# Layer 0's last stage: middle-channel products in four column groups, with one copy and four stores

## The chip, the cores and the metric

The kernel runs on one core of one Trainium2 chip. The metric is device time in microseconds (us) from launch to end; lower is better. The core has a matrix engine (TensorE, PE in the profile), which reads SBUF and writes PSUM, a vector engine (DVE), a scalar engine (ACT), GpSimd (POOL) and a sync engine (SP). SP and POOL are the two that issue DMA transfers here. Each engine runs its own instructions in order; semaphores join them.

## The reference

The model has two layers. Layer 0 ends with an expert-choice channel mixer; layer 1 begins with a Fourier mixer and a linear map `w_f`:

```python
def fourier_mixer(h, w_f):
    b, n, d = h.shape
    hg = h.astype(jnp.float32).reshape(b, n, FNET_GROUPS, d // FNET_GROUPS)
    f = jnp.fft.fftn(hg, axes=(1, 3), norm='ortho').real.reshape(b, n, d).astype(h.dtype)
    return jnp.einsum('bnd,de->bne', f, w_f)

def expert_choice_ffn(x, w_router, w_gate, w_up, w_down):
    b, n, d = x.shape
    t = x.reshape(b * n, d)
    cap = CAPACITY_FACTOR * (b * n) // N_EXPERTS
    aff = jax.nn.softmax(jnp.einsum('td,de->te', t, w_router).astype(jnp.float32), axis=-1)
    g, idx = lax.top_k(aff.T, cap)
    xe = t[idx]
    ...
```

The kernel moves the transform over channels to the weights: it multiplies the channel transform into `w_f` once, long before layer 1 wants it. The channels stand in `GROUPS` = 4 groups of `GW` = 256. A transform of 256 real channels has cosine and sine rows, and one middle row (frequency 128) whose factors are +1, -1, +1, ... over 16. Its products with `w_f` are the "middle channels' mixing weights", `w_f_mid`: one row of D = 1024 numbers for each group, 4 x 1024 in all.

## The kernel before

The program is a row of stages, each a block in which every engine has its own list, with a barrier of all engines between blocks. The stage of the change is `mix0` (function `output_and_choice`). It does layer 0's output projection, the normalised tokens `xh`, the router's logits, and the choice of tokens by each expert (DVE's `rounds`: repeatedly the eight largest of each row). PE has spare time while DVE chooses, and makes the mixing weights there.

`mixing_weight_products` lists these products in order: 16 of 512 columns into `w_f_mixed` (cosine and sine, for four groups and two halves of the columns), and then 2 into `w_f_mid`, one for each half of the columns. Each of the last two is a sum of four matmuls, one for each group g, whose stationary operand `alt_c[:, g, :]` has 4 columns (only column g is not zero) and whose moving operand is `folded[0][:, g, ...]`, 512 columns. The result is 4 rows x 512 in PSUM partitions 0 to 3.

For every product n the same three steps follow one another:
- PE (`mixing_weights`, L1562 to L1572) waits until the product before the last has been copied out, multiplies into one of the two banks of `acc[0]`, and raises `w_full`.
- ACT (`mixing_weights_kept`) waits for `w_full` and for the store that last used the buffer, copies the bank into `stage[n % 4]` (L1652), and raises `w_kept`.
- POOL (L1527 to L1529) waits for `w_kept` and issues a store of that buffer to DRAM, which raises `w_out[n % 4]` when it has landed.

The order at the end of the stage is fixed by the code. PE runs products 11 to 17 and then `choice.turn_lists` (L1255 to L1260), which transposes the chosen lists when DVE's `write_lists` (L1362 to L1366) has raised `lists_ready`. DVE's `write_tables` (L1371 to L1382) turns these into token numbers and raises `tables_ready`; L1382 is its last instruction. POOL, after the 18 stores, waits for `tables_ready` in `fetch_first` and issues two gathers, of the first expert's prompt tokens (L1388) and sample tokens (L1389). Then POOL waits for the landing of all stores (`w_out`), and its list is over. After the barrier the experts' stage begins (`experts`): PE turns the gathered tokens (L1949, L1962), and SP asks for the second expert's weights (L1799).

Two places elsewhere in the program are of use for comparison. Layer 1's mixing stage has a helper `middle` (L2304) which multiplies a stationary operand of one column with 256 moving columns for each quarter of the output columns, with quarter q at PSUM partition 32 q. Layer 1 also has the same chain of lists, tables and gathers at its end, with no stores in POOL's list before it.

Of the kernel before, what the change touches and what calls it, by code (L numbers as in the profile page):

```python
# [29 lines left out]
ACT = mybir.ActivationFunctionType  # L30
# [21 lines left out]
GROUPS = 4  # L52
GW = D // GROUPS
# [5 lines left out]
BANK = 512  # L59
# [46 lines left out]
def wait(eng, sem, value):  # L106

    if not isinstance(value, int) or value > 0:
        eng.wait_ge(sem, value)
# [1315 lines left out]
def output_and_choice(nc, t, per, room, weights):  # L1425
# [4 lines left out]
    with Stage(nc, "mix0") as s:  # L1430
# [10 lines left out]
        acc = [s.ps(f"acc{u}", 2) for u in range(2)]  # L1441
        choice = Choice(s, t, per, 0, [lg[0][:], lg[1][:]], tp, False)
        raw = [s.sb(f"raw{u}", [P, 2, BANK]) for u in range(2)]
        folded = [x[1][:].rearrange("p k f -> p (k f)").rearrange("p (g e) -> p g e", g=GROUPS) for x in (weights.gate, weights.up)]
        stage = [s.sb(f"stage{u}", [P, BANK]) for u in range(4)]
        cos_c, sin_c, odd_c = s.sb("cos_c", [P, HG]), s.sb("sin_c", [P, HG]), s.sb("odd_c", [1, HG])
        alt_c = s.sb("alt_c", [P, GROUPS, GROUPS])
        raw_in, fold_done, chan_in = s.sems("raw_in", 2), s.sem("fold_done"), s.sem("chan_in")
        w_full, w_kept, w_out = s.sem("w_full"), s.sem("w_kept"), s.sems("w_out", 4)
        w_products = list(mixing_weight_products(t["w_f_mixed"], t["w_f_mid"], folded, cos_c[:], sin_c[:], odd_c[:], alt_c[:]))  # L1450
        N_W = len(w_products)

        gate_in, a_in, x_in = s.sem("gate_in"), s.sems("a_in", 2), s.sems("x_in", 2)
# [17 lines left out]
        with nc.Block() as block:  # L1471
# [53 lines left out]
            @block.gpsimd  # L1525
            def _(pool):
                for n, (dst, _) in enumerate(w_products):  # L1527
                    pool.wait_ge(w_kept, n + 1)
                    pool.dma_start(dst, stage[n % 4][0:dst.shape[0], :]).then_inc(w_out[n % 4], 16)  # L1529
                for u in range(2):  # L1530
                    pool.wait_ge(xh_out[u], 16 * NT // 2)
                choice.fetch_first(pool, weights)
                for u in range(4):
                    pool.wait_ge(w_out[u], 16 * ((N_W + 3 - u) // 4))

            @block.tensor
            def _(pe):
                def product(m, half, lo, hi):
                    u = m % 2
                    if half == 0 and lo == 0:  # L1540
                        if m:
                            pe.wait_ge(a_in[u], 32 * ((m + 1) // 2))
                        wait(pe, gated, m - 1)
                    for k in range(lo, hi):
                        last = pe.matmul(acc[u][:, half * BANK:(half + 1) * BANK], a_t[u][:, k, :],
                                         room.row(k)[:, half * BANK:(half + 1) * BANK], start=(k == 0), stop=(k == KD - 1))
                    if half == 1 and hi == KD:
                        last.then_inc(full, 1)

                def turn(m):  # L1550
                    u = m % 2
                    pe.wait_ge(xh_ready, m + 1)
                    for b, kept in ((0, v_kept), (1, a_kept)):
                        wait(pe, kept, m)
                        for j in range(4):
                            k = 4 * b + j
                            last = pe.transpose(tp[b][:, j * P:(j + 1) * P], xh[u][:, k * P:(k + 1) * P], per.ident[:])
                        last.then_inc(tp_full, 1)

                def router(m):  # L1560
                    pe.wait_ge(v_kept, m + 1)
                    pe.wait_ge(a_kept, m + 1)  # L1562
                    choice.route(pe, m // 4, m % 4, xh_t[m % 2])

                def mixing_weights(lo, hi):
                    for n in range(lo, hi):
                        dst, terms = w_products[n]
                        wait(pe, w_kept, n - 1)
                        for m, (stationary, moving) in enumerate(terms):
                            last = pe.matmul(acc[0][0:dst.shape[0], (n % 2) * BANK:(n % 2 + 1) * BANK], stationary, moving,  # L1570
                                             start=(m == 0), stop=(m == len(terms) - 1))
                        last.then_inc(w_full, 1)  # L1572

                pe.wait_ge(room.w_o_in, 32)
                pe.wait_ge(room.first_in, 32)
                product(0, 0, 0, KD)
                product(0, 1, 0, KD)
                choice.make_bias(pe)
                for m in range(1, NT):
                    product(m, 0, 0, KD)  # L1580
                    if m < NT - 1:
                        turn(m - 1)
                        product(m, 1, 0, 4)
                        router(m - 1)
                        product(m, 1, 4, 6)
                        if m in (4, 8):
                            choice.turn_batch(pe, m // 4 - 1)
                        product(m, 1, 6, KD)
                    else:
                        choice.turn_affinities(pe, 1)  # L1590
                        product(m, 1, 0, 4)
                        turn(m - 1)
                        product(m, 1, 4, KD)
                        router(m - 1)
                pe.wait_ge(gated, NT - 1)
                pe.wait_ge(chan_in, 64)
                pe.wait_ge(fold_done, 4 * GROUPS)
                mixing_weights(0, 8)
                turn(NT - 1)
                router(NT - 1)  # L1600
                choice.turn_batch(pe, 2)
                mixing_weights(8, 11)
                choice.turn_affinities(pe, 0)
                mixing_weights(11, N_W)
                choice.turn_lists(pe)

            @block.scalar
            def _(act):
# [38 lines left out]
                def mixing_weights_kept(lo, hi):  # L1647
                    for n in range(lo, hi):
                        rows = w_products[n][0].shape[0]
                        act.wait_ge(w_full, n + 1)  # L1650
                        wait(act, w_out[n % 4], 16 * (n // 4))
                        act.activation(stage[n % 4][0:rows, :], acc[0][0:rows, (n % 2) * BANK:(n % 2 + 1) * BANK], ACT.Copy).then_inc(w_kept, 1)  # L1652
# [10 lines left out]
                choice.keep_batch(act, 2)  # L1663
                choice.exponentials(act, 0)
                mixing_weights_kept(8, N_W)

            @block.vector
            def _(dve):
# [66 lines left out]
                choice.write_tables(dve, ch)  # L1735


def mixing_weight_products(w, w_mid, folded, cos_c, sin_c, odd_c, alt_c):

    for half in range(2):  # L1740
        e = slice(half * BANK, (half + 1) * BANK)
        for g in range(GROUPS):
            yield w[0][g, :, e], [(cos_c, folded[0][:, g, e]), (odd_c, folded[1][0:1, g, e])]
            yield w[1][g, :, e], [(sin_c, folded[1][:, g, e])]
    for half in range(2):
        e = slice(half * BANK, (half + 1) * BANK)
        yield w_mid[:, e], [(alt_c[:, g, :], folded[0][:, g, e]) for g in range(GROUPS)]


class Buffers:  # L1750
# [1054 lines left out]
```

## Time and profile before

| what | value |
|---|---|
| median of 3 runs | 2194.54 us (2191.77 to 2197.46) |
| the profiled execution | 2183.69 us, of which the span from first to last instruction is 2181.9 us |
| PE busy / DVE / ACT / POOL | 2027.1 / 863.0 / 470.3 / 154.6 us |
| end of the stage `mix0` | about 1051.2 us into the span (POOL's last gather) |
| first PE work of the experts' stage | 1056.67 us |

All times in rows are of the profiled execution, in us from the start of its span. A float32 matmul of the program stands as two instructions in the trace, each with a weight load (PEld) ahead of it. A timeline row gives start, length, engine, line, operation, output<-inputs, shape and count; the bracket at its end says how long the engine was idle before, and what ended that. The length of a PE row that merges several matmuls runs to the end of the last one, and the next row can begin before that, since matmuls are pipelined.

### The profile page before, as it was taken

Reading aid. Unit: us, or ns where it says so; the run is one execution under the profiler, and the core shown is the slowest. Engines: PE = TensorE matmul, PEld = TensorE weight load, DVE = VectorE, ACT = ScalarE, POOL = GpSimd, SP = SyncE. Lnnn points to the kernel's source line nnn. Section 1 sums busy time; section 2 is a strip of 40 time slices with the busy share of each in tenths; the row PEclk is TensorE's granted clock in tenths of the full one; section 3 lists DMA queues with packets and bytes.
Section 4 is the critical chain, followed back from the end, with each engine's and each line's share of the span. In section 5 each row is a group of like instructions: output and inputs, shape, how many; then the busy total and the mean of one; then the engine's idle time right before and its main releaser. Section 6 shows DMA issues by size and latency. Waiting matters only on the chain. (4 is left out here: it accounts for less than half of the span.)

```text
span 2181.9 us, 27610 instructions
## 1 busy us (share of the span) xinstructions
PE 2027.1 (93%) x11515; PEld 1430.7 (66%) x11515; DVE 863.0 (40%) x1810; ACT 470.3 (22%) x929; POOL 154.6 (7%) x147
## 2 busy tenths in 40 slices
PE   5999999979999999999799999995998499999998
PEld 2776777755666665443587878783444387878785
DVE  2245445455666664337222222222657522222221
ACT  1222222126665563113000000001222200000000
POOL 0000000000000000001111111111000101111110
PEclk9999999989999999998899999997898699999999
DMA  9201111048444323753767878776221797878782
GB/s 354 94 29 44 43 43 41 25 104 290 176 172 168 136 98 122 264 173 135 268 234 258 305 258 305 248 227 216 99 97 58 277 330 251 302 260 302 261 283 61
DMA packets 159085, 404.29 MB, mean 185 GB/s; under 512 B 12561, under 2 KB 30664, under 8 KB 152818
## 3 DMA queue, kind: packets, MB, share of 16 engines
q1 hardware_dynamic: 142370, 344.30, 43.9%
q0 software_dynamic: 16592, 58.24, 9.3%
q8 instruction: 91, 1.49, 0.3%
q14 instruction: 32, 0.26, 0.0%
HBM read 339.46 MB, written 63.05 MB: 184 GB/s over the span
## 5 line engine op out<-in xcount | busy, mean ns | idle before, releaser
L1970 PE MATMUL experts_gu<-experts_h_t,shared_w_gate 128*128 128x160 f32 x2048 | 303.0, 302 | 4.1 <-issue 4.1
L1970 PEld LDWEIGHTS experts_gu<-experts_h_t,shared_w_gate 128*128 128x128 f32 x2048 | 289.1, 192 | 19.1 <-issue 19.1
L1970 PE MATMUL experts_gu<-experts_h_t,shared_w_up 128*128 128x160 f32 x2048 | 299.7, 300 | 0.0
L1970 PEld LDWEIGHTS experts_gu<-experts_h_t,shared_w_up 128*128 128x128 f32 x2048 | 285.8, 191 | 0.0
L2046 DVE TENSOR_TENSOR experts_hid<-experts_act,experts_gu 128x160 f32<-128x160 f32 x128 | 41.2, 322 | 478.9 <-ACT experts_act L2035 478.9
L1994 PE MATMUL experts_dn<-shared_w_down,experts_hid 128*128 128x512 f32 x512 | 225.9, 594 | 0.0
L523 PE MATMUL proj_cv<-proj_h_t,proj_w_in 128*128 128x256 f32 x960 | 212.4, 379 | 2.6 <-DVE proj_h_t L720 2.6
L2035 ACT ACTIVATE experts_act<-experts_gu 128x160 f32<-128x160 f32 x128 | 38.8, 303 | 813.0 <-PE experts_gu L1970 813.0
L523 PEld LDWEIGHTS proj_cv<-proj_h_t,proj_w_in 128*128 128x128 f32 x960 | 181.8, 191 | 28.6 <-issue 4.7
L1994 PEld LDWEIGHTS experts_dn<-shared_w_down,experts_hid 128*128 128x128 f32 x512 | 94.9, 190 | 113.7 <-issue 113.7
L1008 PE MATMUL attn_sc<-attn_keys_s,attn_q_s 96*128 96x512 f32 (+1 forms) x384 | 154.7, 539 | 3.8 <-DVE attn_pr_t L1141 2.8
L1123 DVE TENSOR_REDUCE attn_least<-attn_sc 128x1 f32<-128x512 f32 (+1 forms) x192 | 109.7, 599 | 101.7 <-PE attn_sc L1008 101.7
L1008 PEld LDWEIGHTS attn_sc<-attn_keys_s,attn_q_s 96*128 96x128 f32 x384 | 67.7, 189 | 90.8 <-issue 64.3
L1074 ACT ACTIVATE attn_pr<-attn_sc,attn_neg 128x1280 f32<-128x1280 f32 x64 | 84.9, 1327 | 128.0 <-DVE attn_neg L1125 128.0
L1081 ACT ACTIVATE attn_pr<-attn_pr,attn_inv 128x512 f32<-128x512 f32 (+2 forms) x144 | 106.3, 785 | 3.5 <-DVE attn_inv L1131 3.5
L516 PE MATMUL proj_lp<-proj_w_in,proj_h_t 128*128 128x384 f32 (+1 forms) x320 | 93.6, 452 | 3.3 <-DVE proj_h_t L720 3.3
L516 PEld LDWEIGHTS proj_lp<-proj_w_in,proj_h_t 128*128 128x128 f32 x320 | 61.6, 193 | 33.3 <-issue 4.9
L1141 DVE COPY attn_pr_t<-attn_sc 128x512 f32<-128x512 f32 x128 | 82.6, 686 | 1.7 <-PE attn_sc L1022 1.7
L1022 PE MATMUL attn_sc<-all_ident,attn_pr 128*128 128x128 f32 x640 | 80.7, 273 | 0.1
L1022 PEld LDWEIGHTS attn_sc<-all_ident,attn_pr 128*128 128x128 f32 x640 | 74.0, 141 | 6.8 <-ACT attn_pr L1081 0.5
L1043 PE MATMUL attn_o<-attn_pr_t,attn_vals_s 128*64 128x128 f32 x1280 | 76.9, 275 | 0.6 <-DVE attn_pr_t L1141 0.6
L1043 PEld LDWEIGHTS attn_o<-attn_pr_t,attn_vals_s 128*64 128x64 f32 x1280 | 69.2, 137 | 6.0 <-issue 5.2
(412 smaller groups left out, 2111.0 us busy)
## 6 DMA issues: line engine op xcount, KB each, us to landing
shared_w_gate<-w_gate_l SPq DMA_DIRECT2D x32, 2048.0 KB, 9.5
shared_w_up<-w_up_l SPq DMA_DIRECT2D x32, 2048.0 KB, 17.3
shared_w_down<-w_down_l SPq DMA_DIRECT2D x32, 2048.0 KB, 22.3
attn_w_mod<-w_mod_l SPq DMA_DIRECT2D x40, 1024.0 KB, 6.6
proj_w_in<-w_in_l SPq DMA_DIRECT2D x3, 2048.0 KB, 19.8
proj_x<-x POOLq DMA_DIRECT2D x10, 512.0 KB, 4.2
shared_w_down<-x SPq DMA_DIRECT2D x10, 512.0 KB, 4.5
layer_room_a<-w_mod_l SPq DMA_DIRECT2D x4, 1024.0 KB, 10.2
```

Source lines behind the costliest of these rows:

```text
L516: last = pe.matmul(lp[:, base:base + hi - lo], h_t[n // 2 % 2][:, k, cols], w_in[:, k, lo:hi], start=(k == 0), stop=(k == KD - 1))
L523: last = pe.matmul(cv[bank][:, j * PAIR:(j + 1) * PAIR], w_in[:, k, base + j * P:base + (j + 1) * P], h_t[p % 2][:, k, :], start=(k == 0), ...
L1008: pe.matmul(sc[b][:, lo:hi], q_s[tile % 2][:, h * P:(h + 1) * P], keys_s[:, h, lo:hi], start=True, stop=True).then_inc(s_full, 1)
L1022: last = pe.transpose(sc[b][:, m * P:(m + 1) * P], pr[b][:, m * P:(m + 1) * P], per.ident[:])
L1043: last = pe.matmul(o_ps[VH * side:VH * (side + 1), base:base + width], vals[:, m, h * VH:(h + 1) * VH], pr_t[n % 4][:, m * width:(m + 1) * ...
L1074: act.activation(pr[b][:], sc[b][:, 0:K], ACT.Exp, bias=neg[b][:, 0:1], scale=-1.0, accum_out=total[b][:, 0:1]).then_inc(p_ready, 1)
L1081: act.activation(pr[b][:, lo:hi], pr[b][:, lo:hi], ACT.Copy, scale=inv[b][:, a:a + 1]).then_inc(p_scaled, 1)
L1123: ch.add(dve.tensor_reduce(least[:, k:k + 1], sc[b][:, lo:hi], AX.X, ALU.min))
L1141: dve.tensor_copy(pr_t[n % 4][:, lo:hi], sc[n % 2][:, lo:hi]).then_inc(v_kept, 1)
L1970: last = pe.matmul(gu[j % 2][:, m * SLOTS:(m + 1) * SLOTS], w[u][:, k, j * P:(j + 1) * P], h_t[u][:, k, :], start=(k == 0), stop=(k == KD ...
L1994: last = pe.matmul(dn[half][:], hid[i][:, k, 0:CAP_S], wd[i][:, k, cols], start=(k == 0), stop=(k == KF - 1))
L2046: dve.tensor_tensor(hid[e % BATCH][:, j, :], act_sb[j % 2][:], gu[j % 2][:, SLOTS:2 * SLOTS], ALU.mult).then_inc(hid_ready, 1)
```

## The change

The two products of `w_f_mid` leave the list of products, which now has 16. PE makes the middle channels in a function of its own, `middle_weights`, after the 16 and still ahead of `turn_lists`. The output columns are cut into four quarters of 256. For each group g there are four matmuls, one for each quarter q, that write PSUM partitions 32 q to 32 q + 3, columns 0 to 255 of one bank. ACT copies all 128 partitions x 256 columns in one instruction; POOL issues four stores of 4 x 256, each raising the new semaphore `mid_out`, and waits for `mid_out` at the very end of its list.

```diff
-        w_full, w_kept, w_out = s.sem("w_full"), s.sem("w_kept"), s.sems("w_out", 4)
-        w_products = list(mixing_weight_products(t["w_f_mixed"], t["w_f_mid"], folded, cos_c[:], sin_c[:], odd_c[:], alt_c[:]))
+        w_full, w_kept, w_out, mid_out = s.sem("w_full"), s.sem("w_kept"), s.sems("w_out", 4), s.sem("mid_out")
+        w_products = list(mixing_weight_products(t["w_f_mixed"], folded, cos_c[:], sin_c[:], odd_c[:]))
...
                     pool.dma_start(dst, stage[n % 4][0:dst.shape[0], :]).then_inc(w_out[n % 4], 16)
+                pool.wait_ge(w_kept, N_W + 1)
+                for q in range(4):
+                    pool.dma_start(t["w_f_mid"][:, q * GW:(q + 1) * GW], stage[N_W % 4][32 * q:32 * q + GROUPS, 0:GW]).then_inc(mid_out, 16)
...
                     pool.wait_ge(w_out[u], 16 * ((N_W + 3 - u) // 4))
+                pool.wait_ge(mid_out, 64)
...
+                def middle_weights():
+                    wait(pe, w_kept, N_W - 1)
+                    for g in range(GROUPS):
+                        for q in range(4):
+                            last = pe.matmul(acc[0][32 * q:32 * q + GROUPS, (N_W % 2) * BANK:(N_W % 2) * BANK + GW], alt_c[:, g, :],
+                                             folded[0][:, g, q * GW:(q + 1) * GW], start=(g == 0), stop=(g == GROUPS - 1), skip_group_check=True)
+                    last.then_inc(w_full, 1)
...
                 mixing_weights(11, N_W)
+                middle_weights()
                 choice.turn_lists(pe)
...
                 mixing_weights_kept(8, N_W)
+                act.wait_ge(w_full, N_W + 1)
+                act.wait_ge(w_out[N_W % 4], 16 * (N_W // 4))
+                act.activation(stage[N_W % 4][:, 0:GW], acc[0][:, (N_W % 2) * BANK:(N_W % 2) * BANK + GW], ACT.Copy).then_inc(w_kept, 1)
...
-    for half in range(2):
-        e = slice(half * BANK, (half + 1) * BANK)
-        yield w_mid[:, e], [(alt_c[:, g, :], folded[0][:, g, e]) for g in range(GROUPS)]
```

On PE, at the end of the stage, before (names are tiles; the shape is that of the output):

```order
501 L1570 MATMUL mix_acc<-shared_w_gate,mix_alt_c 4x512 x8
502 L1255 MATMUL mix_tp<-all_ident,mix_best 128x48
503 L1255 MATMUL mix_tp<-all_ident,mix_lists 128x48 x3
504 L1257 MATMUL mix_tp<-all_ident,mix_at_pf 32x16
505 L1260 MATMUL mix_lg<-all_ident,mix_at_pf 32x4 x4
```

and now, at the same place on PE:

```order
501 L1582 MATMUL mix_acc<-shared_w_gate,mix_alt_c 4x256 x16
502 L1255 MATMUL mix_tp<-all_ident,mix_best 128x48
503 L1255 MATMUL mix_tp<-all_ident,mix_lists 128x48 x3
504 L1257 MATMUL mix_tp<-all_ident,mix_at_pf 32x16
505 L1260 MATMUL mix_lg<-all_ident,mix_at_pf 32x4 x4
```

Nothing has moved around the middle products; 8 matmuls of 512 columns have become 16 of 256, still ahead of the lists (L1255).

On POOL, from the last stores to the two gathers, before:

```order
34 L1529 DMA w_f_mixed<-mix0_stage2 128x512
35 L1529 DMA w_f_mixed<-mix0_stage3 128x512
36 L1529 DMA w_f_mid<-mix0_stage0 4x512
37 L1529 DMA w_f_mid<-mix0_stage1 4x512
38 L1388 DMA shared_w_down3<-xh_prompt,all_at_p4 128x1024
39 L1389 DMA shared_w_down3<-xh_sample,all_at_s 128x1024
```

and now, on POOL:

```order
34 L1529 DMA w_f_mixed<-mix0_stage2 128x512
35 L1529 DMA w_f_mixed<-mix0_stage3 128x512
36 L1532 DMA w_f_mid<-mix0_stage0 4x256 x4
37 L1388 DMA shared_w_down3<-xh_prompt,all_at_p4 128x1024
38 L1389 DMA shared_w_down3<-xh_sample,all_at_s 128x1024
```

Four small stores stand where two stood, and the gathers still come right behind them.

## Rows read from the trace of the kernel before

**Rows 1.** The page, part 1: busy time, share and instructions by engine.

```profile
PE 2027.1 (93%) x11515; PEld 1430.7 (66%) x11515; DVE 863.0 (40%) x1810; ACT 470.3 (22%) x929; POOL 154.6 (7%) x147
```

**Rows 2.** Timeline of DVE, end of `mix0`: start, length, engine, line, operation.

```profile
1039.93 0.22 DVE L1366 CAST mix_lists<-mix_at 48x128 f32<-48x128 uint32 x1
1046.78 0.36 DVE L1371 COPY mix_merge<-mix_tp 128x192 f32<-128x192 f32 x1 [6.62 <-PE mix_lg L1260]
...
1047.84 0.17 DVE L1382 TENSOR_TENSOR all_at_s<-mix_moved,mix_merge 128x16 uint32<-128x16 f32 x1
```

**Rows 3.** Timeline of PE, end of `mix0` and start of the experts.

```profile
1038.95 7.03 PE L1570 MATMUL mix_acc<-shared_w_gate,mix_alt_c 128*4 128x512 f32 x16
1045.91 0.26 PE L1255 MATMUL mix_tp<-all_ident,mix_best 48*128 48x48 f32 x1
...
1056.67 1.94 PE L1949 MATMUL experts_tp<-all_ident,shared_w_down 128*128 128x128 f32 x8 [9.96 <-PEq L1471]
```

**Rows 4.** Timeline of POOL, end of `mix0`.

```profile
1039.94 0.54 POOL L1529 DMA_DIRECT2D w_f_mixed<-mix_stage  x1 [0.52 <-ACT mix_stage L1652]
1043.46 0.52 POOL L1529 DMA_DIRECT2D w_f_mid<-mix_stage  x1 [2.97 <-ACT mix_stage L1652]
1046.89 0.52 POOL L1529 DMA_DIRECT2D w_f_mid<-mix_stage  x1 [2.91 <-ACT mix_stage L1652]
1048.88 1.03 POOL L1388 DMA_INDIRECT shared_w_down<-xh_prompt,all_at_p  x1 [1.46 <-DVE all_at_s L1382]
1050.21 0.97 POOL L1389 DMA_INDIRECT shared_w_down<-xh_sample,all_at_s  x1 [0.30 <-issue]
```

**Rows 5.** Timeline of ACT: the copy of the first middle product.

```profile
1042.58 0.59 ACT L1652 ACTIVATE mix_stage<-mix_acc 4x512 f32<-4x512 f32 x1 [2.93 <-PE mix_acc L1570]
```

**Rows 6.** Layer 1's `middle` (L2304): PE's timeline, then one line's ns min/median/max.

```profile
1664.98 1.04 PE L2304 MATMUL mix_banks<-shared_w_down 128*1 128x256 f32 x16
1665.96 0.61 PE L2304 MATMUL mix_banks<-mix_w_mid,shared_w_down 4*1 4x256 f32 x8
...
L2304 PE MATMUL mix_banks<-shared_w_down x32: 377/378/380, 1661.9 to 1665.7; 128*1 128x256 f32 x32
```

**Rows 7.** ACT's copies of 128 x 256 from PSUM, elsewhere: ns min/median/max.

```profile
L1088 ACT ACTIVATE attn_pr_t<-attn_sc x64: 372/373/383, 511.7 to 841.3; 128x256 f32<-128x256 f32 x64
```

**Rows 8.** Timelines of POOL and DVE elsewhere: small DMAs in a row, waits for DVE.

```profile
5.15 2.03 POOL L202 DMA_DIRECT2D proj_mod_bias<-b_mod_l  x4
...
37.72 0.75 DVE L710 TENSOR_SCALAR proj_xh<-proj_x,proj_rstd 128x1024 f32<-128x1024 f32 x1
...
38.77 0.54 POOL L468 DMA_DIRECT2D proj_x<-x  x1 [26.16 <-DVE proj_xh L710]
...
1719.84 0.18 DVE L1382 TENSOR_TENSOR all_at_s<-mix_moved,mix_merge 128x16 uint32<-128x16 f32 x1
...
1720.82 0.98 POOL L1388 DMA_INDIRECT shared_w_down<-xh_prompt,all_at_p  x1 [22.01 <-DVE all_at_s L1382]
```

**Rows 9.** DMA issues: engine, operation, count, KB each, median us to landing.

```profile
proj_mod_bias<-b_mod_l POOLq DMA_DIRECT2D x4, 4.0 KB, 8.3
...
w_f_mid<-mix_stage POOLq DMA_DIRECT2D x2, 8.0 KB, 1.7
```

**Rows 10.** Windows: us, engines' busy us (instructions), granted PE clock, DMA share, GB/s.

```profile
4.00:9.00 5.00, 0.41 (x2) 0.28 (x2) 0.74 (x3) 1.71 (x4) 3.18 (x6) 1.00 0.72 265
...
1038.95:1045.85 6.90, 6.90 (x17) 1.31 (x16) 1.10 (x5) 1.18 (x2) 1.54 (x3) 1.00 0.19 77
...
1067.00:1068.00 1.00, 1.00 (x5) 1.00 (x5) 0.00 (x0) 0.00 (x0) 0.00 (x0) 0.50 1.05 414
1068.00:1070.00 2.00, 2.00 (x16) 2.00 (x15) 0.00 (x0) 0.07 (x1) 0.00 (x0) 0.97 1.03 398
...
1728.40:1738.00 9.60, 7.55 (x33) 6.73 (x34) 4.45 (x7) 1.24 (x1) 3.01 (x3) 0.54 0.85 282
```

**Rows 11.** Timeline of SP's queue: the experts' stage asks for weights.

```profile
1057.49 0.42 SPq L1799 DMA_DIRECT2D shared_w_gate<-w_gate_l  x1
```

More of the change, by code:

```diff
@@ L1735, in _, with mixing_weight_products @@
                 choice.write_tables(dve, ch)
-def mixing_weight_products(w, w_mid, folded, cos_c, sin_c, odd_c, alt_c):
+def mixing_weight_products(w, folded, cos_c, sin_c, odd_c):
     for half in range(2):
```

## Prediction

> **What bounds the kernel now.** PE is busy 93% of the span [rows 1], but a share over the whole span does not say what the end of one stage waits for. So I read the timelines of the engines at the end of `mix0` side by side, from DVE's last choice to the barrier.
>
> DVE has the chosen lists ready at 1039.93 + 0.22 = 1040.15. Its next instruction begins at 1046.78: it was idle for 6.62 us, and PE released it [rows 2]. PE had not been waiting in that time: it was in the middle products, 16 instructions from 1038.95, and began to turn the lists only at 1045.91 [rows 3]. So from 1040.20 to 1045.91 the choice waits for nothing but PE's order of work. Behind that, in one chain, come the tables, whose last instruction ends at 1047.84 + 0.17 = 1048.01 [rows 2], POOL's two gathers at 1048.88 and 1050.21, the second ending at 1051.18 [rows 4], and 5.49 us after that PE's first work for the experts at 1056.67 [rows 3]. SP asks for the experts' next weights only then, at 1057.49 [rows 11], so the transfers of the next stage move with its start. I found nothing at a fixed time there that would eat a shift; what the end of `mix0` gains should be gained at the end of the kernel.
>
> **PE: the products.** Before, 16 instructions of 512 columns take 1045.91 - 1038.95 = 6.96 us, with the clock fully granted [rows 3, 10]: 0.43 us each and about 0.1 us for the change to the next kind of matmul. 256 columns are half of that, 0.214 us. The new code has 32 instructions of 256 columns, so the same number of columns in all. If the four column groups did not overlap it would win nothing.
>
> Layer 1's `middle` shows the overlap in the same form: four quarters, 256 columns, outputs at partitions 0, 32, 64, 96. Sixteen instructions occupy PE from 1664.98 to 1665.96, 0.98 us [rows 6], where sixteen in turn would need 16 x 0.214 = 3.43. So four run in the time of one, and 0.98 - 4 x 0.214 = 0.12 us is the change of kind. Thirty-two are eight such rounds: 8 x 0.214 + 0.12 = 1.84 us. Their start stays 1038.95, since the wait ahead of them is for the same copy as before. PE then turns the lists at 1040.79, after the lists are ready at 1040.15. Gain at this point: 1045.91 - 1040.79 = 5.12 us.
>
> The Trainium skill ("TensorE: Matmul & The Clock Gate", Part 3, measured speedup) gives less for column packing: three tiles ran 2.38 times as fast, not three times. At the same share four tiles would give 3.17, hence an estimate of 6.86 / 3.17 + 0.12 = 2.28 us in place of 1.84, and a total gain 0.4 us smaller. The row of this kernel shows the full factor; I go by the row.
>
> **DVE.** The turned lists come 5.12 us earlier, so the tables end at 1048.01 - 5.12 = 1042.89.
>
> **ACT: the copy.** Two copies of 0.59 us [rows 5] become one. The last product starts at 1038.95 + 7 x 0.214 + about 0.01 = 1040.46 and lasts 0.378 [rows 6], to 1040.84; ACT began 0.04 us after the end of the first middle product before, so now at 1040.88. 128 x 256 from PSUM took 0.373 us elsewhere [rows 7]: to 1041.25. Its extra wait is for the store of product 12, issued long before; no row shows ACT held by it.
>
> **POOL: the stores, which are the new neighbour of the path.** POOL began a store 0.29 us after the copy ended (1042.58 + 0.59 = 1043.17, then 1043.46) [rows 4, 5], so the first of the four begins at 1041.54; the last old-style store ended at 1040.48 [rows 4], so POOL is free. One middle store took 0.52 us, and four DMAs of 4 KB in a row took 2.03 us [rows 4, 8]. Four stores: 4 x 0.522 = 2.09, to 1043.63. That is 0.74 us after the tables are done, so the gathers no longer wait for DVE, but for POOL's own stores.
>
> What lies between POOL's last store and its first gather, when the semaphore is up already, no row shows. The lower bound is the gap between the two gathers, 0.30 us [rows 4]. The upper one is the whole way from DVE's last instruction to the gather, 0.87 here (1048.01 to 1048.88), and 0.80 in layer 1, where POOL had been idle for 22 us [rows 2, 4, 8]: this way is no effect of queued stores. I take 0.57: of the 0.87 a DVE signal to a plain POOL DMA takes 0.30 (37.72 + 0.75 = 38.47, to 38.77) [rows 8], and a signal that has come already costs nothing.
>
> **The sum.** First gather at 1043.63 + 0.57 = 1044.20, against 1048.88: 4.7 us earlier. With 0.30 it is 4.95, with 0.87 it is 4.4. If the stores were hidden it would be the 5.12 of PE. POOL's last wait, for `mid_out`, is hidden behind the gathers: the last store is issued at 1043.11, a middle store landed 1.7 us after its issue [rows 9], that is 1044.8, and the second gather ends at 1044.20 + 1.03 + 0.30 + 0.97 = 1046.50. If that cover is gone it costs what rival 2 says.
>
> The profiled execution took 2183.69 us (span 2181.9); less 4.7 it is 2179.0 (span 2177.2). It lies 10.9 us under the median shown, so the difference, not its own time, is carried over: 2194.54 - 4.7 = **2189.8 us**. That is 0.21%. About 0.3%, 6.6 us, is what a measurement of this kernel can tell from no change, so the likeliest case is a real gain too small for that bound.
>
> **Rival 1: the column groups do not overlap here.** Then PE needs 32 x 0.214 = 6.86 us as before, and the change does not do what it says. The lists are turned at 1045.91 as before, but the copy now waits for all the products: the last matmul ends at 1045.97, the copy at 1046.38, the four stores at 1048.76, the gather begins at 1049.33, 0.45 us later than before: 2195.0. For it: the stationary operand has four columns here and one in `middle`. Against it: sixteen instructions in 0.98 us in the same form.
>
> **Rival 2: the landing of the stores ends the stage; slower.** POOL must see `mid_out` at 64 before the barrier. Four POOL transfers of 4 KB issued in a row, the very size of the new stores, have a landing of 8.3 us elsewhere [rows 9]. With that the last store lands at 1043.11 + 8.3 = 1051.41, 0.23 us after the old end of POOL's list at 1051.18: 2194.8. The gain begins to shrink at a landing of 1046.50 - 1043.11 = 3.4 us, and is a loss from 8.1 us. For it: same queue, same size. Against it: these 8.3 us stand where the DMA engines are busy 0.72 of the time, at the middle stores it is 0.19 [rows 10], and 8 KB stores from the same place landed in 1.7.
>
> **Rival 3: the clock of the experts' first matmuls.** PE begins the experts at half clock, and the granted clock reads 0.50 to 1068.0 and 0.97 over the next 2 us [rows 10]; so it rises about 11.4 us after 1056.67. In the same place of layer 1 the window of 9.60 us that begins with PE's restart has 0.54 [rows 10]: only some 8% of it, 0.8 us, can be at full clock, so the rise is 8.8 us after the restart. The two differ by 2.6 us. At half clock that is worth 1.3 us. PE is idle for about the same time before the restart in both kernels, so the step itself stays; but when it comes may shift with the start. Earlier, the gain is 6.0 (2188.5); later, 3.4 (2191.1).
>
> **How the numbers follow.** Forecast (a gain of 4.4 to 5.1) 0.74; rival 3 in either direction 0.16, the earlier rise the likelier since this trace has the later one; rival 1 0.04; rival 2 0.06. The three runs of before lie 5.7 us apart, so a median may lie some 2.8 us off. The low end is rival 3's 2188.5 less 2.8, about 2185.5; the high end takes in rivals 1 and 2 at 2195.0 and a little scatter, 2195.5. Faster by over 0.3% needs a gain of 6.6 us: the earlier clock with some scatter, or the forecast with much of it, 0.12. Slower by over 0.3% has no mechanism here that is large enough, only scatter behind rivals 1 and 2: 0.02. Within 0.3%: 0.86.
>
> **What the profile of the changed kernel would show.** For PE's step: the middle products about 1.84 us long from their start to the first matmul of the lists. If it is near 6.9, rival 1 is right. For DVE: the wait ahead of L1371 falls from 6.6 to about 1.5 us. For POOL: four stores back to back, 2.0 to 2.1 us, and the first gather 0.3 to 0.9 us behind the last of them, its idle time put down to POOL's own issue and not to DVE. If it still comes 0.8 us behind DVE's last instruction, the stores were hidden. For rival 2: a landing of `w_f_mid` above 3.4 us, and a longer stretch than 5.5 us from the end of the second gather to PE's first matmul of the experts. For rival 3: where the clock reads 1.00 after that restart. The prediction is wrong if this shift of about 4.7 us stands at the barrier but not at the end of the span.

## Result and the profile after

Four executions of each kernel gave a median of 2182.89 us (2179.72 to 2183.62) for the changed one and 2196.0 us (2191.77 to 2198.36) for the one before: a ratio of 0.994 with a 95% interval of 0.992 to 0.9959. That is 13.1 us, where the prediction had 4.7, and 2182.89 lies 2.6 us under the low end of its range. Yet the two profiled executions have almost the same span, 2181.9 us before and 2181.3 us after. Both need an explanation, and it is the same one. With more executions (experiments 1, 2 and 5) the means are 2190.5 us for 80 executions of before and 2185.2 us for 28 of the changed kernel, a difference of 5.3 us with a 95% interval of 2.9 to 7.7. Without the first four of each it is 4.5 us (1.8 to 7.3). One execution of experiment 7 took 3610.0 us, at a mean granted clock of 0.554, and is left out of its ratio.

First the end of `mix0` in the changed kernel. Timeline of DVE, to be held against [rows 2]:

```profile
1044.48 0.22 DVE L1366 CAST mix_lists<-mix_at 48x128 f32<-48x128 uint32 x1
1046.22 0.36 DVE L1371 COPY mix_merge<-mix_tp 128x192 f32<-128x192 f32 x1 [1.51 <-PE mix_lg L1260]
...
1047.28 0.18 DVE L1382 TENSOR_TENSOR all_at_s<-mix_moved,mix_merge 128x16 uint32<-128x16 f32 x1
```

Timeline of PE, against [rows 3]:

```profile
1043.51 1.91 PE L1582 MATMUL mix_acc<-shared_w_gate,mix_alt_c 128*4 128x256 f32 x32
1045.35 0.26 PE L1255 MATMUL mix_tp<-all_ident,mix_best 48*128 48x48 f32 x1
...
1056.48 1.94 PE L1962 MATMUL experts_tp<-all_ident,shared_w_down 128*128 128x128 f32 x8 [10.33 <-PEq L1471]
```

Timelines of ACT and POOL, against [rows 4, 5]:

```profile
1045.48 0.38 ACT L1681 ACTIVATE mix_stage<-mix_acc 128x256 f32<-128x256 f32 x1 [1.27 <-PE mix_acc L1582]
...
1046.15 2.03 POOL L1532 DMA_DIRECT2D w_f_mid<-mix_stage  x4 [1.11 <-ACT mix_stage L1681]
1048.49 1.02 POOL L1388 DMA_INDIRECT shared_w_down<-xh_prompt,all_at_p  x1 [0.30 <-issue]
1049.82 0.96 POOL L1389 DMA_INDIRECT shared_w_down<-xh_sample,all_at_s  x1 [0.30 <-issue]
```

DMA issues of the stretch 1036 to 1060, median us to landing last, against [rows 9]:

```profile
w_f_mid<-mix_stage POOLq DMA_DIRECT2D x4, 4.0 KB, 1.6
```

The middle products take 1045.35 - 1043.51 = 1.84 us in place of 6.96. DVE waits 1.51 us for the turned lists in place of 6.62. The four stores take 2.03 us, and the first gather begins 0.30 us behind the last of them; the bracket puts that gap down to POOL's own issue and no longer to DVE.

Times of day don't compare here, since the products begin at 1043.51 and not at 1038.95. Counted from their start, the first gather comes after 1048.49 - 1043.51 = 4.98 us, against 9.93 before; the experts' first matmul after 12.97, against 17.72. The stage has become 4.75 us shorter, but in this execution it began 4.56 us later than in the profiled execution of before. That is why the two spans agree.

Why it began later is not the change's doing: the lists of instructions are the same up to this place. The granted clock differs. Windows of before, then the same of the changed kernel (columns as in [rows 10], the granted clock is the third number from the end):

```profile
460.00:520.00 60.00, 45.35 (x209) 29.57 (x208) 34.88 (x79) 28.47 (x68) 0.00 (x0) 0.86 0.86 228
840.00:880.00 40.00, 36.01 (x175) 18.02 (x173) 11.40 (x21) 4.73 (x9) 0.00 (x0) 1.00 0.55 172
1000.00:1036.00 36.00, 31.99 (x95) 11.72 (x94) 31.87 (x78) 13.20 (x22) 6.57 (x13) 0.81 0.49 175
```

```profile
460.00:520.00 60.00, 46.07 (x199) 31.42 (x201) 34.88 (x81) 25.79 (x64) 0.00 (x0) 0.80 0.83 222
840.00:880.00 40.00, 36.00 (x197) 19.66 (x195) 11.91 (x25) 7.94 (x14) 0.00 (x0) 0.91 0.52 166
1000.00:1036.00 36.00, 31.98 (x107) 12.72 (x106) 33.30 (x80) 13.03 (x22) 5.41 (x10) 0.86 0.46 168
```

The clock has two levels, so a mean of 0.80 in 60 us means 24 us at half rate, against 16.8 at 0.86. The changed kernel's execution has 7.2 us more half-rate time in each of the first two windows and 3.6 us less in the third: 10.8 us more, in which PE does at most 5.4 us less work. The stage began 4.56 us later.

The other traces, of both kernels, bear this out. In the clock's records of the eight traces in which PE's order ahead of the middle products is the same, the products start at 1038.33 with 37.5 us of half-rate time ahead of them, 1038.95 with 41.0 (before), 1041.57 with 44.4, 1043.51 with 51.2 (the changed kernel's first), 1043.94 with 54.6 (before again), 1046.88 and 1047.07 with 61.4, and 1049.80 with 64.9: in one order, whichever the kernel.

### The profile page after: what moved, and what is told of

It reads as the page before. It is cut to its first block and busy times, and to the rows that moved or that the text cites. A ratio compares the mean times of both kernels' runs of the same rounds, so it can differ in the third digit from the quotient of the medians.

```text
span 2181.3 us, 27642 instructions
## 1 busy us (share of the span) xinstructions
PE 2028.1 (93%) x11531; PEld 1433.6 (66%) x11531; DVE 862.9 (40%) x1810; ACT 469.6 (22%) x928; POOL 155.0 (7%) x149
```

## Experiments

Theory A: the change is worth 4.7 to 5 us, at the end of `mix0`, and what is more than that between the first medians comes from where half-rate stretches fell in those executions. Theory B: it is worth some 13 us in every execution, by something outside that place.

**1. The kernel before, unchanged, against itself.**

> The kernel before, unchanged, timed against itself, for a second trace and the granted clock of more executions. Theory A (the change is worth 4.7 to 5 us at the end of mix0, and the rest of the 13 us between the medians is where the clock's half-rate stretches happened to fall in the executions compared): executions of this one kernel spread over 8 us or more, between about 2183 and 2198 us, and the longer ones have the lower mean clock, some 0.955 to 0.960 against 0.965 in the profile of before. Theory B (the change is worth some 13 us in every execution, by something outside the end of mix0): the executions lie close to 2196, and the 2183.69 of the profiled one stays the exception. Ratio to the kernel before under both: 1.000.

Measured: ratio 0.9999 (0.9981 to 1.0017). Its 12 executions reach from 2184.29 to 2197.92 us, the 35 of the kernel before beside them from 2183.57 to 2196.96. So one kernel spreads over 13 to 14 us within a set, and the 2183.69 of the first profile is the lower edge of that, not a thing apart. Its trace shows the end of `mix0` as in [rows 2 to 4], 4.99 us later:

```profile
1043.94 7.03 PE L1570 MATMUL mix_acc<-shared_w_gate,mix_alt_c 128*4 128x512 f32 x16
1050.90 0.26 PE L1255 MATMUL mix_tp<-all_ident,mix_best 48*128 48x48 f32 x1
...
1061.47 1.94 PE L1949 MATMUL experts_tp<-all_ident,shared_w_down 128*128 128x128 f32 x8 [9.77 <-PEq L1471]
```

What theory A expected came, its detail on the clock too: sorted by mean granted clock, the executions of both kernels fall in order (76 of before and 28 of the changed kernel that have a listed clock; correlation of time and clock -0.89 and -0.95):

| mean clock | before: executions, mean us | changed: executions, mean us |
|---|---|---|
| 0.957 to 0.959 | 6, 2195.7 | 8, 2192.8 |
| 0.960 | 17, 2195.5 | 3, 2188.6 |
| 0.961 to 0.962 | 13, 2190.5 | 7, 2183.4 |
| 0.963 | 19, 2188.1 | 3, 2182.6 |
| 0.964 | 15, 2186.4 | 4, 2178.5 |
| 0.965 to 0.967 | 6, 2185.3 | 3, 2177.2 |

**2 and 5. The changed kernel, unchanged, twice more.**

> The changed kernel, unchanged, timed once more. Theory A: the ratio comes back between 0.994 and 1.000, nearest to 0.998 (4.7 us of 2195), and at equal mean clock it is 4 to 5 us below the kernel before. Theory B: again 0.994, and also at equal clock some 13 us below.

> The changed kernel once more, unchanged, for twelve more executions and a third trace. Theory A (the gain is made at the end of mix0 alone, and half-rate stretches of PE's clock ahead of the stage make the rest of the difference): from the start of the middle products to the experts' first matmul 12.8 to 13.0 us (17.5 and 17.7 in the two traces of before, 12.8 and 13.0 in those of after), wherever the stage begins; the stage begins the later, the more half-rate time lies ahead of it (1038.95 with 41 us of it, 1047 with 61). Ratio 0.996 to 0.999. Theory B (13 us in every execution): 0.994.

Measured: 0.9975 (0.9955 to 0.9996) and 0.9983 (0.9962 to 1.0004), that is 5.5 and 3.7 us; the second interval takes in 1, and the medians of experiment 5 alone (2189.99 against 2188.6) show no gain. The 13 did not come back. The third trace is a long one (span 2190.3) whose stage begins only at 1049.80, and still it has the same lengths (the experts' first matmul 12.75 us after the products' start; 12.83 in experiment 2's trace):

```profile
1049.80 1.91 PE L1582 MATMUL mix_acc<-shared_w_gate,mix_alt_c 128*4 128x256 f32 x32
1051.64 0.26 PE L1255 MATMUL mix_tp<-all_ident,mix_best 48*128 48x48 f32 x1
...
1062.55 1.94 PE L1962 MATMUL experts_tp<-all_ident,shared_w_down 128*128 128x128 f32 x8 [10.11 <-PEq L1471]
```

Two traces of before have 17.72 and 17.53, three of the changed kernel 12.97, 12.83 and 12.75: 4.8 us by the means. From there to the end of the span it is 1125.2 and 1127.6 us before, 1124.8, 1125.1 and 1127.8 after: these lengths scatter by 3 us, and within that nothing of the gain is given back or added.

One length does not repeat. In this third trace DVE waits 5.68 us for the turned lists and not 1.51:

```profile
1052.51 0.36 DVE L1371 COPY mix_merge<-mix_tp 128x192 f32<-128x192 f32 x1 [5.68 <-PE mix_lg L1260]
```

There PE, at half rate from 1020 to 1047 by the clock's records, is still at the 16 products ahead of the middle ones when DVE has its lists at 1046.83. The end of the stage hangs on PE in either case, which is why lengths counted from the start of the middle products compare and DVE's wait does not.

The expectation of experiment 2 missed in one point: at equal mean clock the table's rows differ by 2.9 to 8.1 us, not by 4 to 5. One slope for both kernels puts the difference at 6.8 us (6.0 to 7.7). The mean clock also counts half-rate time in which PE is idle and which costs nothing. Between the start of the middle products and the experts' first matmul that is 5.6 and 5.2 us in the traces of before and 7.7, 7.5 and 8.5 in those of the change, by the clock's records. So at equal mean clock the changed kernel has some 2.5 us less of the half-rate time that does cost. By an estimate from these figures, 2.5 us at half rate are worth 1.25 us, and 4.8 + 1.25 = 6.05. What is left is less than 1 us, and the interval reaches down to it.

**3. No overlap: the loops exchanged.**

```diff
-                    for g in range(GROUPS):
-                        for q in range(4):
+                    for q in range(4):
+                        for g in range(GROUPS):
```

> The changed kernel with the two loops of the middle products exchanged: the four groups of one quarter follow one another in one column group, so neighbours can't overlap; same number of instructions, same copy, same four stores. Both theories: the middle products take 6.9 us in place of 1.84, and the first gather comes 9.2 to 9.7 us after DVE's lists (8.7 in before, 3.8 in after), since the copy now waits for all 32. Theory A: 0.2 to 0.8 us slower than before, ratio 1.000. Theory B with a cause in the stores or in the one copy and not in the overlap: still well below 1, 0.995 to 0.997.

Measured: ratio 0.9981 (0.9965 to 0.9998).

```profile
1046.88 4.50 PE L1582 MATMUL mix_acc<-shared_w_gate,mix_alt_c 128*4 128x256 f32 x32
1051.31 0.26 PE L1255 MATMUL mix_tp<-all_ident,mix_best 48*128 48x48 f32 x1
...
1054.42 1.02 POOL L1388 DMA_INDIRECT shared_w_down<-xh_prompt,all_at_p  x1 [0.30 <-issue]
```

The expectation failed: 4.43 us, not 6.9. Windows of 0.2 us of these matmuls alone show why (the first number with an x is PE's busy time, and the x counts the instructions in flight in the window):

```profile
1047.26:1047.46 0.20, 0.20 (x2) 0.09 (x1) 1.00 0.00 0
...
1048.26:1048.46 0.20, 0.20 (x6) 0.07 (x3) 1.00 0.94 389
...
1050.66:1050.86 0.20, 0.20 (x3) 0.07 (x1) 1.00 0.00 0
```

At first one instruction follows another, with two in a window (each lasts 0.379 us and the next begins 0.21 us after it); in the middle there are up to six. The length tells the same: 4.43 us are about 20 steps of 0.214 and the change of kind, where 32 in turn would need 32 steps, and 29 if only the last instruction of a quarter ran beside the first of the next. The starts in the trace are four alone, then twelve pairs, then four alone. The records do not name the quarter, but 20 steps come out if each quarter of eight begins beside the fifth instruction of the one before it, although it comes later in the list. So the experiment reduces the overlap, from four at a time to two at most, and does not remove it.

It still gives a second point: the gather comes 1054.42 - 1046.88 = 7.54 us after the start, 2.56 us later than with full overlap, and PE's step has grown by 2.59. The one copy and the four stores are the same here, so it is the overlap that carries the gain. The time can't tell this kernel from the changed one.

**4. The gathers ahead of the stores on POOL.**

```diff
+                for u in range(2):
+                    pool.wait_ge(xh_out[u], 16 * NT // 2)
+                choice.fetch_first(pool, weights)
                 pool.wait_ge(w_kept, N_W + 1)
                 for q in range(4):
                     pool.dma_start(t["w_f_mid"][:, q * GW:(q + 1) * GW], stage[N_W % 4][32 * q:32 * q + GROUPS, 0:GW]).then_inc(mid_out, 16)
-                for u in range(2):
-                    pool.wait_ge(xh_out[u], 16 * NT // 2)
-                choice.fetch_first(pool, weights)
```

> The changed kernel with POOL's two gathers ahead of the four small stores, so that the stores are off the way from the tables to the gathers. The first gather should come 0.8 to 0.9 us after DVE's last table instruction (1.21 in after), that is 0.3 to 0.4 us earlier than in after. The stores then end 2.1 us after the second gather, and the last one lands 1.6 us after its issue. If the end of POOL's list sets the barrier, the experts start 2 to 3 us later than in after; if the landing of the gathers sets it (4.2 and 5.4 us), they start 0.3 us earlier. Time against after: between 0.4 us shorter and 3 us longer, so a ratio of 0.998 to 0.999 to before in theory A.

Measured: ratio 0.9975 (0.9955 to 0.9995), in time no different from the change itself.

```profile
1047.07 1.91 PE L1582 MATMUL mix_acc<-shared_w_gate,mix_alt_c 128*4 128x256 f32 x32
...
1050.83 0.18 DVE L1382 TENSOR_TENSOR all_at_s<-mix_moved,mix_merge 128x16 uint32<-128x16 f32 x1
1051.88 1.04 POOL L1388 DMA_INDIRECT shared_w_down<-xh_prompt,all_at_p  x1 [3.28 <-DVE all_at_s L1382]
1053.22 0.97 POOL L1389 DMA_INDIRECT shared_w_down<-xh_sample,all_at_s  x1 [0.30 <-issue]
1054.19 2.11 POOL L1535 DMA_DIRECT2D w_f_mid<-mix_stage  x4
...
1061.44 1.94 PE L1962 MATMUL experts_tp<-all_ident,shared_w_down 128*128 128x128 f32 x8 [11.74 <-PEq L1471]
```

The gather comes 4.81 us after the start of the products: the stores on the way cost only 4.98 - 4.81 = 0.17 us, less than the 0.3 to 0.4 expected. The expectation had counted 1.21 us from the start of DVE's last instruction and 0.8 to 0.9 from its end; from its end it is 1.03 in the change and 0.87 here.

The experts begin after 14.37 us, 1.5 later than in the change. What they wait for has to be read with care. They follow the end of POOL's last issue (1054.19 + 2.11 = 1056.30) by 5.14 us here, and by 5.3 to 5.7 in the traces where the gathers come last, but that is no fixed way. By the landings in the traces, the experts follow the landing of the second gather by 1.15 us in both traces of before and by 1.23 in all three of the change and in experiments 3 and 7. So there the landing of that gather sets the start; [rows 4] end with its issue, and its landing, 5.3 us after it began, comes later than the 1051.2 at which the table of the kernel before puts the end of the stage. The landings of the second gather, first before, then in the change (the last number):

```profile
shared_w_down<-xh_sample,all_at_s POOLq DMA_INDIRECT x1, 5.3
...
shared_w_down<-xh_sample,all_at_s POOLq DMA_INDIRECT x1, 5.4
```

Here the second gather has landed 3.1 us before the experts begin, and something else is last. The landing of `w_f_mid`, for which POOL waits at the end of its list, takes longer than the 1.6 us of the change:

```profile
DMA to landing us min/median/max: 3.2/3.3/3.6
```

The last store lands at 1059.01. POOL's own records show its wait for the stores ending at 1059.04, and behind it a drain, an instruction at the end of the block, to 1061.15, 0.29 us ahead of the experts' first matmul. In the change the same wait is over at 1049.28, while the gathers are being issued. So the landing of the stores does end the stage when they stand behind the gathers, and is covered when they stand ahead of them: that is where they belong.

**6. The lists turned first on PE, and the stores on SP.**

```diff
                 mixing_weights(11, N_W)
-                middle_weights()
                 choice.turn_lists(pe)
+                middle_weights()
...
+                sp.wait_ge(w_kept, N_W + 1)
+                for q in range(4):
+                    sp.dma_start(t["w_f_mid"][:, q * GW:(q + 1) * GW], stage[N_W % 4][32 * q:32 * q + GROUPS, 0:GW]).then_inc(mid_out, 16)
+                sp.wait_ge(mid_out, 64)
```

(The four stores and the wait for `mid_out` are gone from POOL.)

> The changed kernel with the lists turned ahead of the middle products on PE, and with the four stores issued by SP in place of POOL, so that neither stands between DVE's lists and the gathers. First gather 0.05 + 2.1 + 0.87 = 3.0 us after DVE's lists (3.8 in after) where PE is at the middle products before the lists are ready, and the experts' first matmul as much earlier, if SP's stores land before the gathers do. In time 0.8 us or less against after, 0.04%, too small for the clock of these executions to show; the trace decides. If SP's stores land late, behind the gathers, the experts start later instead, as with the gathers ahead of the stores (14.4 us after the start of the middle products in place of 12.9).

Measured: ratio 0.9972 (0.9954 to 0.999), median 2182.12 us.

```profile
1045.43 0.22 DVE L1366 CAST mix_lists<-mix_at 48x128 f32<-48x128 uint32 x1
...
1045.71 0.26 PE L1255 MATMUL mix_tp<-all_ident,mix_best 48*128 48x48 f32 x1 [0.19 <-DVE mix_lists L1366]
...
1046.43 1.91 PE L1582 MATMUL mix_acc<-shared_w_gate,mix_alt_c 128*4 128x256 f32 x32
1056.28 1.94 PE L1962 MATMUL experts_tp<-all_ident,shared_w_down 128*128 128x128 f32 x8 [7.93 <-PEq L1471]
...
1048.68 1.03 POOL L1388 DMA_INDIRECT shared_w_down<-xh_prompt,all_at_p  x1 [1.70 <-DVE all_at_s L1382]
```

As expected, the gather comes 1048.68 - 1045.65 = 3.03 us after DVE's lists, and the experts 10.63 us after them, against 11.78 in the change's first trace and 11.62 in its second. By the trace this is another 1.0 to 1.2 us, where 0.8 was expected; the timed runs can't tell it from the change.

**7. The middle products made twice.**

```diff
-                    for g in range(GROUPS):
+                    for g in [*range(GROUPS), *range(GROUPS)]:
```

> The changed kernel with the sixteen middle matmuls made twice (the second pass overwrites the first), all else the same: the step on PE doubled by itself. Column groups that fully overlap cost 8 x 0.214 = 1.72 us more: middle products 3.55 us, and gather and experts 1.7 us later than in after, 14.6 us from the start of the middle products to the experts. If the groups overlapped less over a longer run, the step would grow by more than 1.72. In time 1.7 us above after.

Measured: ratio 0.9979 (0.9961 to 0.9997).

```profile
1038.33 3.64 PE L1582 MATMUL mix_acc<-shared_w_gate,mix_alt_c 128*4 128x256 f32 x64
1041.90 0.26 PE L1255 MATMUL mix_tp<-all_ident,mix_best 48*128 48x48 f32 x1
...
1052.75 1.94 PE L1962 MATMUL experts_tp<-all_ident,shared_w_down 128*128 128x128 f32 x8 [10.06 <-PEq L1471]
```

The products take 3.57 us, 1.73 more, and the gather and the experts come later by 1.73 and about 1.6 us (14.42 against 12.85). Full overlap holds over 64 instructions, and what PE spends here is passed on to the experts almost whole: it is on the path. The 1.7 us expected in time don't show: the mean of the 11 executions is 2184.4 us, against 2185.2 for the changed kernel.

## Why the prediction failed, and what of it held

The mechanism held, step by step, and the size of the gain nearly so.
- PE: 1.84 us predicted, 1.84 measured. Experiment 7 gives 8 x 0.214 + 0.02 for 32 instructions more. The estimate of 2.28 from the Trainium skill ("TensorE: Matmul & The Clock Gate", Part 3, measured speedup), worked out from its lower factor for packed columns, is not borne out here.
- DVE's wait: 1.5 predicted, 1.51 in the first trace. The copy 0.373 and 0.38. POOL's first store 0.29 us behind the copy (1045.86 to 1046.15). The stores 2.09 and 2.03.
- From the last store to the gather 0.57 predicted, 0.30 in all three traces of the change: this term of the sum was mis-sized, and its lower bound was right. The gain at the gather is 9.93 - 4.98 = 4.95, the upper end of the forecast's 4.4 to 5.1.
- The shift came through to the experts with 4.8 us and, within the 3 us by which the lengths behind it scatter, to the end of the span. The prediction let the experts follow POOL's last gather at a fixed 5.49 us; it is the gather's landing that they follow (experiment 4), which costs or gives some 0.2 us from trace to trace.
- Rival 1: refuted by the 1.84. Rival 2: the stores landed 1.6 us after issue, so its 3.4 us were not reached; its path is real, as experiment 4 shows. Rival 3: the clock rose 9.4 us after the restart in the changed kernel's first trace, against 11.4, but from the restart to the end of the span that trace is only 0.4 us shorter (1124.8 against 1125.2), and the 12.0 of its third trace lie on the other side.

What failed is the base of the sum and its spread, in "How the numbers follow". The prediction took the three runs shown for the spread of the kernel, let a median be 2.8 us off, and carried the gain over to 2194.54. The kernel before has a median of 2189.3 over 80 executions, so the base was 5.2 us too high: with 2189.3 the sum gives 2184.6, and 2182.89 is 1.7 us below that. Medians of four drawn at random from the executions now known of each kernel differ with a standard deviation of 4.7 us; 4 draws of 100 differ by 13.1 or more. That is how the first comparison reads: all four executions of before lie in the longer half of what that kernel does, and all four of the changed one below the median of 2185.8 of its later 24. So most of the 13.1 us is the luck of that draw, as far as these executions tell. The two later sets, from two chips, have means of 2190.7 and 2189.4 us for the kernel before; on which chip the first comparison ran the record doesn't say.

The sign had been in view: the profiled execution lay 10.9 us under the median, outside the three runs. The prediction read that as an offset to be carried, where it was a sample of the spread. With twice 4.7 us for the scatter the low end would have stood near 2180.4, and 40 of 100 such draws differ by more than 6.6 us, where the prediction gave 0.12.

## What to carry to other kernels

Small products that wait at the end of a stage can be packed into column groups at a full factor of four when the group changes with every instruction; what counts is then the next queue behind PE, here POOL's, so put the small stores where that queue is waiting anyway, and ahead of the larger transfers whose landing covers theirs. Read a change of a few microseconds from the traces, by lengths counted from a common event inside the stage, and not from the spans. Before a range is set, take any execution outside the few runs shown as a measure of the spread: here one kernel's executions lie 14 us apart.

## What the runs showed of the hardware that was not expected

Matmuls of one column group hold back those of the next group behind them in the list only in part: with eight instructions in a row for each group the 32 took 4.43 us, two at a time in the middle, where one after another would be 6.86 and a change of group at every instruction took 1.84 (experiment 3).

POOL's four small stores took 1.6 us to land ahead of two gathers and 3.2 to 3.6 us behind them (experiment 4).

The time from PE's restart after the barrier to full clock varies from execution to execution of the same kernel. After the experts' first matmul at 1056.48 the clock of the changed kernel's first trace is back within the window that ends at 1066, 9.4 us on:

```profile
1064.00:1066.00 2.00, 2.00 (x10) 2.00 (x9) 0.00 (x0) 0.00 (x0) 0.00 (x0) 0.54 1.04 418
1066.00:1068.00 2.00, 2.00 (x17) 2.00 (x16) 0.00 (x0) 0.00 (x0) 0.00 (x0) 1.00 1.03 409
```

In experiment 5's trace of the same kernel, whose first matmul is at 1062.55, it is 12.0 us (0.86 in a window of 2 us is 1.4 us at full rate):

```profile
1072.00:1074.00 2.00, 2.00 (x10) 2.00 (x9) 0.00 (x0) 0.00 (x0) 0.00 (x0) 0.50 1.03 408
1074.00:1076.00 2.00, 2.00 (x14) 2.00 (x14) 0.00 (x0) 0.00 (x0) 0.00 (x0) 0.86 1.02 396
```

The trace of before, with 11.4 [rows 10], lies between them. What sets the moment in one execution these runs don't show.
